# State-space norm and mixed output: where the second 128 tokens' transposes stand, and VectorE's order around them

## The chip, the cores and the metric

The kernel runs on one core of one Trainium2 chip. The metric is the device time of one execution in microseconds (us), the median of several runs.

## What is computed

The kernel computes two transformer blocks over 256 tokens of 1024 features. The first has a stick-breaking and a retention head mix, a mixture of 32 experts and a gated side input; the second has attention, a state-space branch, a gated mix of both and a dense feed-forward part. The change lies in the second block, between the state-space branch and the feed-forward part. Cut to that:

```python
def second_block(x, ...):
    ...
    attn_out = gqa_attention(q, k, v) @ w_attn_proj[i]
    ssd_y = ssd_branch(...)          # ends in rms_norm(y * silu(z), ssd_norm)
    ssd_out = ssd_y @ w_ssd_proj[i]
    g_attn, g_ssd = jnp.split(jax.nn.sigmoid(gates), N_BRANCH, axis=-1)
    mixed = (g_attn * attn_out + g_ssd * ssd_out) @ w_out[i]
    x = x + rms_norm(mixed, norm1_post[i])
    h2 = rms_norm(x, norm2_pre[i])
    gate, up = jnp.split(h2 @ w_gate_up[i], 2, axis=-1)
    ffn = (jax.nn.silu(gate) * up) @ w_down[i]
    return x + rms_norm(ffn, norm2_post[i])
```

## The kernel before

**Products in three parts.** Every large product is made from a high and a low part of both sides: `product` (L518) issues high by high (L520), high by low (L521) and low by high (L522). For weights ScalarE makes the high part of a piece (`split`, L1207, instruction L1210) and GpSimd the low part (L2163, four instructions of 128x512 for a piece of 1024 KB). For the activations, which TensorE transposes into PSUM, ScalarE copies the high part into XNT[0] and VectorE subtracts it from the PSUM value into XNT[1], the low part.

**Pieces and release.** The weights come in pieces in a fixed order: attn_proj 0 and 1, then ssd_proj (0,0), (0,1), (1,0), (1,1), out2 in the same four, then gate 0, up 0, gate 1 and so on. SP loads them into eight slots; `split_to(n)` makes ScalarE split all pieces up to number n, and each split waits (`w_used`) until TensorE is done with the piece four places ahead of it. `split_to` stands at fixed places of ScalarE's program, so its position among the other instructions sets when GpSimd gets a piece. GpSimd takes the pieces in order, each when its high part is there (`w_high`).

**The two blocks of tokens.** The 256 tokens are two blocks of 128, tb 0 and tb 1. `pair_group` (L589) makes one group of 512 output columns: for tb 0 both halves of the inner dimension (12 + 12 matmuls of 128x512), then the same for tb 1. It waits for the two weight pieces (`arrived`, on GpSimd's `w_low`) and, through `need_chunk`, for the low parts of its own block (`xnT` or `mixT`). The pieces are released in tb 1's turn.

**The state-space norm.** VectorE makes the normed rows NY (`norm(4, Y, NY)`, L2089, instruction L1543) one block after the other, with ScalarE's sum of squares (L1222) and root (L1224) ahead of each. TensorE's `norm_T(4)` is `block_transposes` (L534, instruction L539): for each block it waits for `xn` and transposes eight chunks into four PSUM banks from bank 0 on, with one increment of `xnT_ps` for four chunks. ScalarE's `block_evac` (L1241, instruction L1246) makes eight high parts for a block, VectorE's (L1558, instruction L1564) eight low parts. Between the norm and its low parts VectorE multiplies the attention's product by its gate, a column half at a time (L2094, `attn_out`): this reads PSUM banks 4 to 7, which ssd_proj's products then overwrite, and so TensorE waits for `attn_out` at 2 ahead of the first of them (L1132). On ScalarE the split for ssd_proj (1,0) stands ahead of the high parts, and those for (1,1) and out2 behind them.

**The mixed output.** When ssd_proj's rows of a block are complete (`first_rows` at 3 for tb 0, `w_used` for tb 1), VectorE multiplies them by their gate (L2101) and adds the attention's part (L2102, `mixed`). TensorE transposes both blocks (`block_transposes(XN, 0, "mixT_ps", "mixed", 0)`, L1135), ScalarE copies four high parts of 128x512 (L1478) and VectorE subtracts for four low parts (L2103 to L2105, instruction L1547). The products of out2 follow (L1137, L1138).

**Behind it.** ScalarE takes the squares of out2's first block (L1494), VectorE scales it (L2111) and adds it to x (L2112), then the squares of the new x (L1222), the other half of the second block (L1486) and so on lead to the next norm and to the feed-forward part.

Nothing is planned at run time: every engine follows its own written order, and semaphores hold them together.

Of the kernel before, what the change touches and what calls it, by code (L numbers as in the profile page):

```python
# [17 lines left out]
ALU = mybir.AluOpType  # L18
# [5 lines left out]
NTB = T // P  # L24
D = 1024
# [45 lines left out]
V_MIX, V_FFN, V_PLE, V_SSD, V_N1, V_N2 = (i * KC for i in range(6))  # L71
# [57 lines left out]
def build_program(nc, a, out):  # L129
# [5 lines left out]
    pieces, number = [], {}  # L135
# [41 lines left out]
    place = {k: n if n < late else n - late + base_c for k, n in number.items()}  # L177
# [18 lines left out]
    with ExitStack() as ctx:  # L196
# [5 lines left out]
        def sem(name):  # L202
            return sems[name]
# [40 lines left out]
        def area(at, n, parts=P):  # L244
            return arena[0:parts, at:at + n]

        def t3(ap, b):
            return ap.rearrange("p (b n) -> p b n", b=b)

        def banks(b, n):  # L250
            return PS[:, b:b + n, :].rearrange("p b n -> p (b n)")
# [6 lines left out]
        def pair(name, at_high, at_low, cols):  # L258
            return (parts_at(name + "_h", arena_byte + 4 * at_high, cols), parts_at(name + "_l", arena_byte + 4 * at_low, cols))

        X = area(0, 2048)
        XN = area(2048, 2048)
        XNT = pair("XNT", 4096, 6144, 2048)
# [62 lines left out]
        NY = area(8192, 2048)  # L326
# [45 lines left out]
        def block_part(ap, b):  # L372

            tb, h = divmod(b, 2)
            return ap.rearrange("p (c b n) -> p b c n", c=KC, b=NTB)[:, tb, 4 * h:4 * h + 4]
# [15 lines left out]
        NORM_BANK = (4, 4, 4, 4, 0, 0)  # L391
# [120 lines left out]
        def _(pe):  # L512
            def arrived(key):
                pe.wait_ge(sem("w_low"), number[key] + 1)
                if number[key] < FIRST_LOW:
                    pe.wait_ge(sem("first_low"), number[key] + 1)
# [7 lines left out]
            def transposes(src, bank, sem_name, ready, base):  # L524

                for tb in range(NTB):
                    pe.wait_ge(sem(ready), base + tb + 1)
                    for c in range(KC):
                        ins = nc.tensor.transpose(PS[:, bank + c // 2, (c % 2) * 256 + tb * P:(c % 2) * 256 + (tb + 1) * P],
                                                  t3(src, 2)[:, tb, c * P:(c + 1) * P], ident)  # L530
                        if tb == 1 and c % 2:
                            ins.then_inc(sem(sem_name), 1)

            def block_transposes(src, bank, sem_name, ready, base):  # L534

                for tb in range(NTB):
                    pe.wait_ge(sem(ready), base + tb + 1)
                    for c in range(KC):
                        ins = nc.tensor.transpose(PS[:, bank + 2 * tb + c // 4, (c % 4) * P:(c % 4 + 1) * P],  # L539
                                                  t3(src, 2)[:, tb, c * P:(c + 1) * P], ident)  # L540
                        if c % 4 == 3:
                            ins.then_inc(sem(sem_name), 1)
# [9 lines left out]
            def norm_T(i):  # L552
                if i == 1:
                    transposes(X, NORM_BANK[i], "xnT_ps", "x1", 0)
                elif i == 2:
                    block_transposes(X, NORM_BANK[i], "xnT_ps", "x2", 0)
                else:
                    by = block_transposes if i in (3, 4) else transposes
                    by(NY if i == 4 else XN, NORM_BANK[i], "xnT_ps", "xn", 2 * i)
# [3 lines left out]
            def takes(name, base, by_block=False):  # L563

                T_ready[:] = name, base, by_block
# [20 lines left out]
                                  [x[:, k, :] for x in w], start=c == first, stop=c == last)  # L586
                return ins

            def pair_group(tag, g, lhs, bank_of, first_rows=False):  # L589

                for tb in range(NTB):
                    for h in range(2):
                        arrived((tag, g, h))
                        ins = group_rows((tag, g, h), lhs, h, tb, bank_of(tb))
                        if tb == 1:
                            ins.then_inc(sem("w_used"), 1)
                        elif h == 1 and first_rows:
                            ins.then_inc(sem("first_rows"), 1)
# [514 lines left out]
            for v in range(len(UNITS)):  # L1113
                if v in FILL:
                    g, half = divmod(FILL.index(v), 2)
# [11 lines left out]
            half_group("attn_proj", 0, None, ATTT, lambda tb: 4 + tb, last=3)  # L1127
            pe.wait_ge(sem("across"), 8)
            half_group("attn_proj", 1, None, ATTT, lambda tb: 6 + tb, last=3)
            norm_T(4)  # L1130
            takes("xnT", 16, True)
            pe.wait_ge(sem("attn_out"), 2)  # L1132
            pair_group("ssd_proj", 0, XNT, lambda tb: 4 + 2 * tb)
            pair_group("ssd_proj", 1, XNT, lambda tb: 5 + 2 * tb, first_rows=True)
            block_transposes(XN, 0, "mixT_ps", "mixed", 0)  # L1135
            takes("mixT", 0, True)
            pair_group("out2", 0, XNT, lambda tb: 4 + 2 * tb)  # L1137
            pair_group("out2", 1, XNT, lambda tb: 5 + 2 * tb, first_rows=True)  # L1138

            norm_T(5)  # L1140
# [34 lines left out]
        def _(act):  # L1175
            link, _n = chain(act, "act_step")
# [15 lines left out]
            for at, name in SWAPPED:  # L1192
                dst, src = (x.rearrange("o (i b j) -> o i b j", i=2, b=2) for x in (bc[0:1, at:at + HD], a[name]))
# [44 lines left out]
                                                   ACT.Copy, scale=vecT[:, gain + c:gain + c + 1])  # L1238
                    ins.then_inc(sem("xnT_high"), 1)

            def block_evac(i, gain):  # L1241
                for tb in range(NTB):
                    for h in range(2):
                        act.wait_ge(sem("xnT_ps"), 4 * i + 2 * tb + h + 1)
                        for c in range(4 * h, 4 * h + 4):
                            ins = nc.scalar.activation(XNT[0][:, c * 256 + tb * P:c * 256 + (tb + 1) * P],  # L1246
                                                       PS[:, NORM_BANK[i] + 2 * tb + h, (c % 4) * P:(c % 4 + 1) * P],
                                                       ACT.Copy, scale=vecT[:, gain + c:gain + c + 1])
                        ins.then_inc(sem("xnT_high"), 1)
# [207 lines left out]
            for v in range(len(UNITS)):  # L1457
# [5 lines left out]
                if v - 1 in (FILL[1], FILL[3]):  # L1463
                    g = FILL.index(v - 1) // 2
# [6 lines left out]
            act.dma_start(N1P, a["norm1_post_2"].to_broadcast([P, D])).then_inc(sem("post1_in"), 16)  # L1471
            split_to(number[("attn_proj", 1)] + 3)
            act.wait_ge(sem("xn"), 2 * 4 + 2)
            block_evac(4, V_SSD)
            split_to(number[("ssd_proj", 1, 1)] + 2)
            for b in range(4):
                act.wait_ge(sem("mixT_ps"), b + 1)
                nc.scalar.activation(block_part(XNT[0], b), PS[:, b, :].rearrange("p (c n) -> p c n", c=4), ACT.Copy).then_inc(sem("mixT_high"), 1)  # L1478
            act.dma_start(N2P, a["norm2_post_2"].to_broadcast([P, D])).then_inc(sem("post2_in"), 16)
# [54 lines left out]
        def _(dve):  # L1534
            link, count = chain(dve, "dve_step")
            V = nc.vector
            tt, ts, stt = V.tensor_tensor, V.tensor_scalar, V.scalar_tensor_tensor
# [7 lines left out]
            def low(out, value, high):  # L1545

                return tt(out, value, high.bitcast(F32), ALU.subtract)  # L1547
# [7 lines left out]
                                  vecT[:, gain + c:gain + c + 1], XNT[0][:, cols].bitcast(F32), ALU.mult, ALU.subtract)  # L1555
                    ins.then_inc(sem("xnT"), 1)

            def block_evac(i, gain):  # L1558
                for tb in range(NTB):
                    for h in range(2):  # L1560
                        dve.wait_ge(sem("xnT_high"), 4 * i + 2 * tb + h + 1)
                        for c in range(4 * h, 4 * h + 4):
                            cols = slice(c * 256 + tb * P, c * 256 + (tb + 1) * P)
                            ins = stt(XNT[1][:, cols], PS[:, NORM_BANK[i] + 2 * tb + h, (c % 4) * P:(c % 4 + 1) * P],  # L1564
                                      vecT[:, gain + c:gain + c + 1], XNT[0][:, cols].bitcast(F32), ALU.mult, ALU.subtract)
                        ins.then_inc(sem("xnT"), 1)
# [485 lines left out]
            g4 = GATES.rearrange("p (b n) -> p b n", b=2)  # L2052
# [38 lines left out]
            for g in range(2):  # L2091
                dve.wait_ge(sem("w_used"), place[("attn_proj", g)] + 1)
                part = g4[:, :, g * 512:(g + 1) * 512]
                tt(part, part, PS[:, 4 + 2 * g:6 + 2 * g, :], ALU.mult).then_inc(sem("attn_out"), 1)  # L2094
            dve.wait_ge(sem("attn_out"), 2)
            block_evac(4, V_SSD)

            for tb, (name, n) in enumerate((("first_rows", 3), ("w_used", place[("ssd_proj", 1, 1)] + 1))):
                dve.wait_ge(sem(name), n)
                mix = XN[:, tb * D:(tb + 1) * D]  # L2100
                link(tt(mix, banks(4 + 2 * tb, 2), g4[:, tb, D:2 * D], ALU.mult))  # L2101
                tt(mix, mix, g4[:, tb, 0:D], ALU.add).then_inc(sem("mixed"), 1)  # L2102
            for b in range(4):  # L2103
                dve.wait_ge(sem("mixT_high"), b + 1)
                low(block_part(XNT[1], b), PS[:, b, :].rearrange("p (c n) -> p c n", c=4), block_part(XNT[0], b)).then_inc(sem("mixT"), 1)  # L2105

            def post_first(i, gain, signal):

# [84 lines left out]
```

## Time and profile before

| | us |
|---|---|
| median of 3 runs | 1630.44 |
| lowest and highest | 1629.87, 1630.76 |
| the profiled execution's own time | 1630.89 |
| its span | 1629.1 |
| TensorE busy in the span | 1477.9 (91%) |
| VectorE, ScalarE, GpSimd busy | 470.1, 421.2, 459.9 |

All times of a trace are in us from the start of the span. A table of windows has for each stretch: its bounds and length, then for TensorE's matmuls (PE), TensorE's weight loads (PEld), VectorE (DVE), ScalarE (ACT) and GpSimd (POOL) the busy time and the number of instructions in brackets, then the granted clock of TensorE as a share of 2.4 GHz, the share of the DMA engines and what they moved. A timeline row has start, duration, engine, line, operation, what is written from what, and the number of instructions; the bracket at its end is how long the engine sat idle ahead of it, and what ended that. The chain of waits has start, duration and the work that stood on the path. L520, L539, L1210, L1246, L1547 and L1564 are lines of helpers that several stages use, so the time tells which stage a row belongs to.

### The profile page before, as it was taken

How to read it: one execution, taken by the hardware profiler on the slowest of the kernel's cores; microseconds unless marked ns; L12 is line 12 of the kernel's file. 1: busy time of each engine (PE TensorE's matmuls, PEld its weight loads, DVE VectorE, ACT ScalarE, POOL GpSimd, SP SyncE). 2: the span in 40 equal slices, each digit the busy share in tenths (PEclk: the TensorE clock that was granted, in tenths of full speed). 3: DMA queues.
4: the chain of work that ended last, by engine and by line, in shares of the span. 5: the costliest groups of instructions: out<-in, count | busy, mean ns of one | idle time of the engine just before them, and what ended most of it. 6: DMA issues, size and time to landing. Idle time of an engine off the chain costs nothing.

```text
span 1629.1 us, 18659 instructions
## 1 busy us (share of the span) xinstructions
PE 1477.9 (91%) x7547; PEld 843.5 (52%) x7548; DVE 470.1 (29%) x806; ACT 421.2 (26%) x530; POOL 459.9 (28%) x356
## 2 busy tenths in 40 slices
PE   6998999998888989888888999887999998989998
PEld 5866633333333323333333333333798776789986
DVE  5526511211111111111111111112266286333311
ACT  5364310100101001001010010103555643354332
POOL 5924100000000000000000000003588563769994
PEclk9999899999999999999999999999999999989999
DMA  9531599999999999999999999999465331635540
GB/s 344 184 103 52 225 429 426 428 427 428 427 428 427 428 428 428 427 428 427 428 428 426 428 427 428 429 427 351 136 190 173 104 104 65 195 128 185 188 171 26
DMA packets 91171, 502.26 MB, mean 308 GB/s; under 512 B 7835, under 2 KB 38163, under 8 KB 66387
## 3 DMA queue, kind: packets, MB, share of 16 engines
q1 hardware_dynamic: 89600, 498.71, 75.8%
q10 hardware_dynamic: 1491, 2.36, 0.5%
q8 instruction: 65, 1.06, 0.3%
q14 instruction: 15, 0.12, 0.0%
HBM read 500.00 MB, written 1.05 MB: 308 GB/s over the span
## 4 chain that ended last, share of the span: by engine, by line
PE 54%; DMA 34%; DVE 5%; ACT 3%; issue 2%; POOL 1%; SPq 1%; ACTq 1%; DVEq 0%
DMA ring<-in_w_up_gate 33%; PE PS L841 14%; PE PS L520 10%; PE PS L522 9%; PE PS L521 9%; PE PS L859 4%; PE PS L810 1%; POOL w_low L2163 1%; DMA ring<-in_w_ple_gate 1%; PE PS L1094 1%; SPq L422 1%; ACT w_high L1210 1%; PE PS L848 0%; DVE arena L1843 0%; DVE arena L1846 0%
## 5 line engine op out<-in xcount | busy, mean ns | idle before, releaser
L2163 POOL TENSOR_TENSOR w_low<-ring,w_high 128x512 fp32r<-128x512 f32 (+1 forms) x352 | 459.6, 1341 | 1148.0 <-ACT w_high L1210 1147.1
L841 PE MATMUL PS<-ring,arena 128*64 128x512 f32 x2048 | 459.6, 600 | 35.4 <-DMA ring<-in_w_up_gate 35.3
L841 PEld LDWEIGHTS PS<-ring,arena 128*64 128x64 f32 x2048 | 142.3, 138 | 336.5 <-issue 268.5
L859 PE MATMUL PS<-ring,arena 128*64 128x512 f32 x1024 | 231.9, 606 | 28.0 <-ACT arena L1347 28.0
L1338 ACT ACTIVATE arena<-arena 128x512 f32<-128x512 f32 x32 | 20.1, 630 | 765.9 <-DVE arena L1840 765.9
L1210 ACT ACTIVATE w_high<-ring 128x2048 fp32r<-128x2048 f32 (+1 forms) x89 | 166.3, 1882 | 115.8 <-PE PS L522 101.3
L859 PEld LDWEIGHTS PS<-ring,arena 128*64 128x64 f32 x1024 | 74.3, 139 | 163.5 <-issue 163.5
L1840 DVE TENSOR_SCALAR arena<-PS 128x512 f32<-128x512 f32 x32 | 22.1, 692 | 470.3 <-PE PS L841 470.3
L520 PE MATMUL PS<-w_high,XNT_h 128*128 128x512 f32 (+1 forms) x336 | 135.7, 404 | 6.8 <-DVE XNT_l L1564 5.2
L520 PE MATMUL PS<-XNT_h,w_high 128*128 128x256 f32 (+1 forms) x464 | 132.2, 285 | 2.9 <-DVE XNT_l L1554 1.9
L522 PE MATMUL PS<-w_high,XNT_l 128*128 128x512 f32 (+1 forms) x336 | 132.4, 394 | 0.0
L521 PE MATMUL PS<-w_low,XNT_h 128*128 128x512 f32 (+1 forms) x336 | 132.4, 394 | 0.0
L521 PE MATMUL PS<-XNT_l,w_high 128*128 128x256 f32 (+1 forms) x464 | 131.8, 284 | 0.0
L522 PE MATMUL PS<-XNT_h,w_low 128*128 128x256 f32 (+1 forms) x464 | 131.8, 284 | 0.0
L1849 DVE COPY arena<-PS 128x512 f32<-128x512 f32 x32 | 22.1, 692 | 279.0 <-PE PS L859 279.0
L520 PEld LDWEIGHTS PS<-XNT_h,w_high 128*128 128x128 f32 (+1 forms) x464 | 87.3, 188 | 3.9 <-issue 2.5
L521 PEld LDWEIGHTS PS<-XNT_l,w_high 128*128 128x128 f32 (+1 forms) x464 | 87.4, 188 | 0.4
L522 PEld LDWEIGHTS PS<-XNT_h,w_low 128*128 128x128 f32 (+1 forms) x464 | 87.3, 188 | 0.3
L520 PEld LDWEIGHTS PS<-w_high,XNT_h 128*128 128x128 f32 x336 | 64.2, 191 | 23.2 <-issue 6.8
L521 PEld LDWEIGHTS PS<-w_low,XNT_h 128*128 128x128 f32 x336 | 64.1, 191 | 14.5 <-issue 0.7
L522 PEld LDWEIGHTS PS<-w_high,XNT_l 128*128 128x128 f32 x336 | 63.8, 190 | 14.9
L866 PE MATMUL PS<-arena 64*128 64x512 f32 x256 | 63.6, 615 | 0.0
(353 smaller groups left out, 1444.8 us busy)
## 6 DMA issues: line engine op xcount, KB each, us to landing
ring<-in_w_up_gate SPq DMA_DIRECT2D x128, 2048.0 KB, 24.3
ring<-in_w_down SPq DMA_DIRECT2D x64, 2048.0 KB, 22.2
ring<-in_w_in SPq DMA_DIRECT2D x35, 1024.0 KB, 5.9
ring<-in_w_gate_up SPq DMA_DIRECT2D x22, 1024.0 KB, 5.1
ring<-in_w_down SPq DMA_DIRECT2D x11, 1024.0 KB, 4.9
ring<-in_w_out SPq DMA_DIRECT2D x8, 1024.0 KB, 5.0
ring<-in_w_ple_gate SPq DMA_DIRECT2D x4, 1024.0 KB, 22.3
ring<-in_w_ssd_proj SPq DMA_DIRECT2D x4, 1024.0 KB, 5.0
```

Source lines behind the costliest of these rows:

```text
L422: sp.dma_start(slot(s)[:, 0:chunks * width].rearrange("p (k n) -> p k n", k=chunks), src).then_inc(landed[s], 16)
L520: nc.tensor.matmul(out, lhs[0], rhs[0], start=start, stop=False)
L521: nc.tensor.matmul(out, lhs[0], rhs[1], start=False, stop=False)
L522: return nc.tensor.matmul(out, lhs[1], rhs[0], start=False, stop=stop)
L841: ins = nc.tensor.matmul(PS[64 * (n % 2):64 * (n % 2) + 64, 4 + n // 2, :], x, w[:, n * 512:(n + 1) * 512], start=False, stop=c == KC - 1, ...
L859: ins = nc.tensor.matmul(PS[64 * n:64 * n + 64, 7, :], lhs, w[:, k, n * 512:(n + 1) * 512], start=(j, k) == (0, 0), stop=(j, k) == (1, 3))
L866: ins = nc.tensor.matmul(PS[:, 2 * tb + n, :], SPT[64 * n:64 * n + 64, tb * P:(tb + 1) * P], YS[64 * n:64 * n + 64, :], start=False, stop= ...
L1210: nc.scalar.activation(HIGH[m % BUF][:, 0:size(key)], slot(raw_slot(key))[:, 0:size(key)], ACT.Copy).then_inc(sem("w_high"), 1)
L1338: nc.scalar.activation(SIG, GLU, ACT.Sigmoid, scale=1.702).then_inc(sem(sig_out), 1)
L1840: ts(GLU, PS[:, 4, :], 7.0, None, ALU.min).then_inc(sem("glu"), 1)
L1849: V.tensor_copy(YS, PS[:, 7, :]).then_inc(sem("y_slots"), 1)
L2163: ins = nc.gpsimd.tensor_tensor(LOW[raw_slot(key)][:, at], slot(raw_slot(key))[:, at], HIGH[m % BUF][:, at].bitcast(F32), ALU.subtract)
```

## The change

TensorE: `block_transposes` takes the blocks that it is to do. The norm's first block is transposed ahead of ssd_proj's first group, the second between that group's tb 0 and tb 1; the wait for `attn_out` is split, 1 ahead of tb 0, and 2 ahead of tb 1. The mixed output's first block is transposed ahead of out2's first group, its second between tb 0 and tb 1.

ScalarE: the split for ssd_proj (1,1) comes between the high parts of the two blocks, and the splits for out2 (1,0) and (1,1) between the second and the third high part of the mixed output.

VectorE: gate product 0, the first block's low parts, gate product 1, the second block's low parts. For the mixed output: multiply and add of tb 0, multiply of tb 1, two low parts, add of tb 1, two low parts. The computation is the same.

```diff
-            def block_transposes(src, bank, sem_name, ready, base):
+            def block_transposes(src, bank, sem_name, ready, base, blocks=range(NTB)):
-                for tb in range(NTB):
+                for tb in blocks:
...
-            def pair_group(tag, g, lhs, bank_of, first_rows=False):
+            def pair_group(tag, g, lhs, bank_of, first_rows=False, between=None):
                 for tb in range(NTB):
+                    if tb == 1 and between:
+                        between()
...
-            norm_T(4)
+            def norm_4_rows(tb):
+                block_transposes(NY, NORM_BANK[4], "xnT_ps", "xn", 8, (tb,))
+
+            def second_rows():
+                norm_4_rows(1)
+                pe.wait_ge(sem("attn_out"), 2)
+
+            norm_4_rows(0)
             takes("xnT", 16, True)
-            pe.wait_ge(sem("attn_out"), 2)
-            pair_group("ssd_proj", 0, XNT, lambda tb: 4 + 2 * tb)
+            pe.wait_ge(sem("attn_out"), 1)
+            pair_group("ssd_proj", 0, XNT, lambda tb: 4 + 2 * tb, between=second_rows)
             pair_group("ssd_proj", 1, XNT, lambda tb: 5 + 2 * tb, first_rows=True)
-            block_transposes(XN, 0, "mixT_ps", "mixed", 0)
+            block_transposes(XN, 0, "mixT_ps", "mixed", 0, (0,))
             takes("mixT", 0, True)
-            pair_group("out2", 0, XNT, lambda tb: 4 + 2 * tb)
+            pair_group("out2", 0, XNT, lambda tb: 4 + 2 * tb,
+                       between=lambda: block_transposes(XN, 0, "mixT_ps", "mixed", 0, (1,)))
...
             act.wait_ge(sem("xn"), 2 * 4 + 2)
-            block_evac(4, V_SSD)
+            block_evac(4, V_SSD, (0,))
+            split_to(number[("ssd_proj", 1, 1)])
+            block_evac(4, V_SSD, (1,))
             split_to(number[("ssd_proj", 1, 1)] + 2)
             for b in range(4):
+                if b == 2:
+                    split_to(number[("out2", 1, 1)])
                 act.wait_ge(sem("mixT_ps"), b + 1)
...
                 tt(part, part, PS[:, 4 + 2 * g:6 + 2 * g, :], ALU.mult).then_inc(sem("attn_out"), 1)
+                block_evac(4, V_SSD, (g,))
             dve.wait_ge(sem("attn_out"), 2)
-            block_evac(4, V_SSD)
...
+            mix_times(0)
+            mix_plus(0)
+            mix_times(1)
+            mix_low(0)
+            mix_low(1)
+            mix_plus(1)
+            mix_low(2)
+            mix_low(3)
```

## Rows read from the trace of the kernel before

**Rows 1.** Table of windows, all engines, the stretches around the change and the rest.

```profile
core 0: us, PE busy (x) PEld busy (x) DVE busy (x) ACT busy (x) POOL busy (x), PEclk, DMA share, GB/s
1367.70:1373.50 5.80, 2.22 (x18) 1.75 (x17) 5.17 (x10) 5.61 (x15) 2.40 (x2) 1.00 0.70 270
...
1397.50:1401.10 3.60, 1.90 (x18) 1.66 (x16) 3.36 (x4) 1.25 (x3) 0.00 (x0) 1.00 1.08 365
1401.10:1423.50 22.40, 22.40 (x99) 17.89 (x96) 5.23 (x6) 10.63 (x13) 19.60 (x16) 1.00 0.48 153
...
1434.90:1629.10 194.20, 188.53 (x1320) 176.07 (x1320) 47.28 (x47) 71.77 (x58) 161.66 (x124) 0.98 0.42 141
```

**Rows 2.** Chain of waits, 1369.9 to 1373.5 us: start, duration, work.

```profile
1369.93 2.27 DVE arena L2094 x2
1372.22 1.14 DVE XNT_l L1564 x4
```

**Rows 3.** Timeline of ScalarE and TensorE at the state-space norm.

```profile
1369.10 1.92 ACT L1210 ACTIVATE w_high<-ring 128x2048 fp32r<-128x2048 f32 x1 [0.16 <-issue]
1370.93 4.21 ACT L1246 ACTIVATE XNT_h<-PS,vecT 128x128 fp32r<-128x128 f32 x16
...
1369.98 1.09 PE L539 MATMUL PS<-cst,arena 128*128 128x128 f32 x8 [0.42 <-DVE arena L1543]
1373.50 0.47 PE L520 MATMUL PS<-w_high,XNT_h 128*128 128x512 f32 x1 [2.42 <-DVE XNT_l L1564]
```

**Rows 4.** Timeline at an earlier norm with the same helpers, ScalarE and VectorE.

```profile
1134.84 4.23 ACT L1246 ACTIVATE XNT_h<-PS,vecT 128x128 fp32r<-128x128 f32 x16
...
1136.09 4.23 DVE L1564 SCALAR_TENSOR_TENSOR XNT_l<-PS,vecT,XNT_h 128x128 fp32r<-128x128 f32 x16 [2.61 <-ACT XNT_h L1246]
```

**Rows 5.** Timeline at the mixed output: TensorE, VectorE, ScalarE.

```profile
1397.50 1.03 PE L539 MATMUL PS<-cst,arena 128*128 128x128 f32 x8
1400.24 1.09 PE L539 MATMUL PS<-cst,arena 128*128 128x128 f32 x8 [1.70 <-DVE arena L2102]
1401.09 0.48 PE L520 MATMUL PS<-w_high,XNT_h 128*128 128x512 f32 x1
...
1398.96 1.22 DVE L2102 TENSOR_TENSOR arena<-arena 128x1024 f32<-128x1024 f32 x1
...
1401.57 1.29 DVE L1547 TENSOR_TENSOR XNT_l<-PS,XNT_h 128x512 fp32r<-128x512 f32 x2 [0.18 <-ACT XNT_h L1478]
...
1400.94 0.60 ACT L1478 ACTIVATE XNT_h<-PS 128x512 fp32r<-128x512 f32 x1 [1.71 <-PE PS L539]
```

**Rows 6.** Timeline behind out2's first products, and adds elsewhere: GpSimd, ScalarE, VectorE.

```profile
1403.90 20.06 POOL L2163 TENSOR_TENSOR w_low<-ring,w_high 128x512 fp32r<-128x512 f32 x16 [7.14 <-ACT w_high L1210]
...
1409.77 1.92 ACT L1210 ACTIVATE w_high<-ring 128x2048 fp32r<-128x2048 f32 x1 [4.14 <-PE PS L522]
...
1425.07 1.06 ACT L1222 ACTIVATE arena<-arena 128x1024 f32<-128x1024 f32 x1 [4.59 <-DVE arena L2112]
...
1426.46 0.58 ACT L1486 ACTIVATE arena<-PS 128x512 f32<-128x512 f32 x1
...
1393.37 2.24 DVE L2102 TENSOR_TENSOR arena<-arena 128x1024 f32<-128x1024 f32 x1
...
1421.29 3.75 DVE L2112 TENSOR_TENSOR arena<-arena 128x1024 f32<-128x1024 f32 x1
...
1620.99 1.22 DVE L2112 TENSOR_TENSOR arena<-arena 128x1024 f32<-128x1024 f32 x1
```

**Rows 7.** Table of windows, columns as in Rows 1, for the granted clock.

```profile
1374.10:1377.20 3.10, 3.10 (x9) 2.39 (x8) 2.35 (x10) 2.83 (x6) 2.17 (x3) 0.50 0.00 0
...
157.10:162.20 5.10, 1.09 (x8) 0.86 (x8) 3.58 (x4) 2.54 (x6) 5.10 (x5) 1.00 0.00 0
162.30:165.40 3.10, 3.10 (x7) 2.46 (x8) 3.07 (x2) 0.00 (x0) 3.10 (x2) 0.50 0.00 0
...
1401.10:1405.00 3.90, 3.90 (x20) 3.17 (x18) 1.57 (x3) 3.90 (x4) 1.10 (x1) 1.00 0.74 237
```

More of the change, by code:

```diff
@@ L1239, in norm_evac, with block_evac @@
                     ins.then_inc(sem("xnT_high"), 1)
-            def block_evac(i, gain):
-                for tb in range(NTB):
+            def block_evac(i, gain, blocks=range(NTB)):
+                for tb in blocks:
                     for h in range(2):
@@ L1556, in norm_evac, with block_evac @@
                     ins.then_inc(sem("xnT"), 1)
-            def block_evac(i, gain):
-                for tb in range(NTB):
+            def block_evac(i, gain, blocks=range(NTB)):
+                for tb in blocks:
                     for h in range(2):
@@ L2094, in _, with mix_times, mix_plus, mix_low @@
                 tt(part, part, PS[:, 4 + 2 * g:6 + 2 * g, :], ALU.mult).then_inc(sem("attn_out"), 1)
+                block_evac(4, V_SSD, (g,))
             dve.wait_ge(sem("attn_out"), 2)
-            block_evac(4, V_SSD)
-            for tb, (name, n) in enumerate((("first_rows", 3), ("w_used", place[("ssd_proj", 1, 1)] + 1))):
+            def mix_times(tb):
+                name, n = (("first_rows", 3), ("w_used", place[("ssd_proj", 1, 1)] + 1))[tb]
                 dve.wait_ge(sem(name), n)
+                link(tt(XN[:, tb * D:(tb + 1) * D], banks(4 + 2 * tb, 2), g4[:, tb, D:2 * D], ALU.mult))
+            def mix_plus(tb):
                 mix = XN[:, tb * D:(tb + 1) * D]
-                link(tt(mix, banks(4 + 2 * tb, 2), g4[:, tb, D:2 * D], ALU.mult))
                 tt(mix, mix, g4[:, tb, 0:D], ALU.add).then_inc(sem("mixed"), 1)
-            for b in range(4):
+            def mix_low(b):
                 dve.wait_ge(sem("mixT_high"), b + 1)
                 low(block_part(XNT[1], b), PS[:, b, :].rearrange("p (c n) -> p c n", c=4), block_part(XNT[0], b)).then_inc(sem("mixT"), 1)
+            mix_times(0)
[6 more added lines that the diff above has]
+            mix_low(3)
             def post_first(i, gain, signal):
```

## The prediction

> **What bounds the kernel now.** The change touches two short stretches of the second block, so the question is what ends last there, not which engine is busiest over the span. I read the table of windows first [rows 1]: between 1367.7 and 1373.5 us TensorE has no products for 5.80 us (the norm), between 1397.5 and 1401.1 none for 3.60 us (the mixed output). The products that follow each stretch run without a gap: 96 in 22.40 us, 0.233 us apart. From 1434.9 on TensorE is busy for 188.5 of 194.2 us, so what is gained or lost before that point reaches the end one for one.
>
> Then the chain of waits through the first stretch [rows 2]: the two gate products on VectorE (L2094, 2.27 us), then four low parts (L1564, 1.14 us), then TensorE at 1373.50. Read alone this says that VectorE is last. The timeline of the other engines beside it [rows 3] says more: ScalarE makes the high parts from 1370.93 on, right behind a weight split of 1.92 us that began at 1369.10. TensorE's second eight transposes (1369.98) lie in time in which it would wait anyway: they are free.
>
> **The change, part by part.** In the norm TensorE now transposes only the first 128 tokens, waits for one gate product, makes the first tokens' 24 products, and then transposes the second 128 tokens. VectorE does one gate product, eight low parts, the other gate product, eight low parts.
>
> Start of the first products. The second gate product goes from ahead of the low parts to behind them, which takes half of 2.27 us, 1.1 us, off VectorE's chain. What is late next: the low parts also wait for four high parts. At another norm with nothing in VectorE's way its low parts begin 1.25 us after ScalarE's high parts [rows 4]. Here that is 1370.93 + 1.25 = 1372.18, and they began at 1372.22 [rows 2]. So ScalarE is behind VectorE by 0.04 us only, and the start moves by at most that: I take 0. Its split and its first high parts are where they were.
>
> The hole behind the first 24 products. The eight transposes now stand between products, and the second tokens' products need their high and low parts, which nothing has made ahead. From transposes to ScalarE's first copy: 1400.94 - 1400.24 = 0.70 us [rows 5]; high to low 1.25 [rows 4]; low to product 1373.50 - 1372.22 = 1.28 [rows 2, 3]. Sum 3.2 us, of which some 0.9 us are the transposes and 2.4 us a wait. Before, this work stood under the first tokens' products. Cost: +3.2 us. Bounds: 0.9 us, were the copies somehow covered, and 3.3 us with the first hand-off at 1.29. I take 3.2: all three terms are rows of the same instructions. The second gate product (1.1 us) is behind the first eight low parts and is over well before; the wait for it costs nothing, since some 5.6 us of products cover it. ScalarE's split for ("ssd_proj", 1, 1) moves ahead of the second tokens' high parts, into the time of the first products; its piece has its use only two groups on, so GpSimd's work for it changes nothing.
>
> Start of out2. Before, TensorE sent eight transposes at 1397.50, waited for the second multiply and add on VectorE, sent eight more at 1400.24 and began at 1401.09: 3.59 us [rows 5]. Now the add of the second tokens is behind two low parts. VectorE is free of the multiply at 1398.96 (1.46 us in). The high part is there by then: 0.70 us for the hand-off and 0.6 for the copy, 1.3 us. The low part takes 0.66 us (two in 1.29), the hand-off to TensorE 0.14 (1.28 less the 1.14 of the four low parts [rows 2]): 1.46 + 0.66 + 0.14 = 2.26 us. Gain: -1.33 us. The add, 1.2 to 2.2 us [rows 6], follows the second low part and has the rest of 5.6 us of products as cover.
>
> The hole in out2. Transposes again stand between the first and the second tokens: 0.70 + 0.63 to the low part + 0.66 + 0.14 = 2.1 us [rows 2, 5] of delay for TensorE. Whether it reaches the end hangs on what follows. After out2's first tokens ScalarE takes squares, and VectorE adds x (L2112). That add began 20.2 us after out2's first product, took 3.75 us, and was over at 1425.04; the same instruction at the end of the kernel took 1.22 [rows 6]. In between GpSimd had 16 low-part instructions in one row from 1403.90, 20.06 us long, to 1423.96, and the add ends 1.08 us after it. So it waited for GpSimd, and ScalarE's next square waited for it (4.59 us idle [rows 6]). The change makes the splits for ("out2", 1, 0) and (1, 1) earlier, between high parts 1 and 2, so that GpSimd is through with both before it needs the next. It then waits for ("gate", 0), whose split followed its release at 8.68 us after the first product (1409.77); with the hole at 10.8, plus 1.92 for the split, GpSimd starts at 12.8, and eight instructions of 1.254 us (20.06 over 16) end at 22.8. The add is due at 20.2 + 2.1 = 22.3, waits 0.5 us and ends 1.08 us after GpSimd: at 23.9, and before it was 23.95. TensorE's own end, 22.4 + 2.1 = 24.5 plus 0.3 for the hand-off, is ahead of ScalarE's L1486, which stood at 25.4 [rows 6]. So the second hole is covered by a wait that shrinks. Cost: 0; without this cover, 2.1 us.
>
> The Trainium skill (SBUF — State Buffer, section on two separate sides) says that a VectorE instruction with two SBUF inputs and a GpSimd one that reads SBUF lock the port, and "the other fully blocks". The trace agrees for L2112, but by the row at 1393.37, 2.24 us, one can also get through between GpSimd's instructions; were the port shared instead of locked, the add would still be slow for its 0.5 us of overlap only.
>
> The Trainium skill (TensorE: Matmul & The Clock Gate, section on each phase of a matmul) says that TensorE pulls weight loads ahead and that matmuls "themselves stay in program order". That speaks against this change: no product of the second tokens could pass the transposes. The trace shows the same, each L539 group with products strictly behind it; the sum above has no overlap in it.
>
> SP's loads wait for the pieces' release and shift with TensorE; no load is moved past another.
>
> **The sum.** 3.23 - 1.33 + 0 = +1.9 us. On the profiled execution, 1630.89 us (span 1629.1), that is 1632.8; that execution is 0.45 us above the median of 1630.44, so 1632.3 us as the median.
>
> **Rivals.** (a) *The clock falls in the new hole.* The granted clock went to 0.50 (1.2 GHz) for 3.1 us behind the norm, and so it did after 157.1 to 162.2 us, where TensorE had eight transposes in 5.1 us; in and after the 3.6 us at 1397.5, with sixteen, it stayed at 1.00 [rows 1, 7]. The new hole has eight transposes in 3.2 us, shorter than any with a drop, but with more idle time (2.4 us) than the one without (1.7). At half the clock products take up to twice as long, so 3.1 us of it cost up to 1.55 us: I take 1.5, so 1633.8. The longer wait ahead of the first products may also bring the present drop forward from 1374.1 to 1373.5, 0.3 us more.
>
> (b) *The x add isn't relieved.* GpSimd would have to run as far past the add's start as before, for instance because its two pieces for out2 are not earlier; the hole of 2.1 us then counts: 1634.4. It decides from the point where GpSimd's last low part ends over 3 us behind the add's start. Against it: the release of ("gate", 0) fixes GpSimd's end. With (a) as well, 1635.8.
>
> (c) *The holes are hidden, and VectorE was last.* Then the transposes alone move (+0.9), the second gate product saves 1.1 and out2 starts 1.33 earlier: -1.6 us, 1628.9. For it: the chain names VectorE. Against it: 1372.18 for ScalarE, and copies that can't begin before the transposes. Only a saving of twice that would be measured as faster.
>
> **How the numbers follow.** A measurement of this kernel can tell about 0.2% (3.3 us) from no change. Forecast 0.52; (a) alone 0.24; (b) alone 0.12; both 0.05; (c) 0.07. Slower by over 0.2% are (b), both, half of (a), and a little of the forecast's own spread (0.03): 0.32. Faster: 0.04, from (c) with more than I can find. Within: 0.64. The range is 1630.8 to 1634.9: below, the forecast with the spread of the runs and a hole that is 1 us shorter; above, (a) and (b) singly with 0.5 us. It leaves out (c) and both together.
>
> **What would show it.** Right: the first product of ssd_proj still about 1.3 us behind the first low part; L539 in four groups, each pair with products between; an idle time of TensorE of some 2.3 us ahead of ssd_proj's second tokens and 1.2 ahead of out2's; out2 starting 2.3 us after its transposes; L2112 at 1.6 us instead of 3.75. Wrong: first products over 0.5 us earlier relative to the norm's end, a hole under 2 us, a granted clock of 0.50 right behind the new hole, or L2112 still over 3 us.

## The result, and the profile after

The changed kernel takes 1634.25 us (median of 14 runs, 1631.97 to 1635.82) where the kernel before takes 1630.72 in the same comparison (14 runs, 1629.51 to 1632.51). The ratio is 1.0018, 95% interval 1.0011 to 1.0025: 2.9 us slower, 1.8 to 4.1. (The two medians lie 3.5 us apart, the two means 3.1. Every "ratio" below is the recorded estimate with its interval, and a difference in us of whole times is worked out from it.) The time lies inside the range of the prediction and within the 0.2% that was called no change; the difference is 1.0 us above the forecast of 1.9. By the interval the change costs something, and it gains nothing.

The profiled execution of the changed kernel took 1635.04 us, with a span of 1633.2. To see what the change did in it, I take the stretch from the state-space norm's first normed rows (VectorE, L1543 before, L1557 after) to the feed-forward part's second normed rows (L2134, L2164). Everything that the change touches lies inside. Timeline of VectorE, the kernel before, start and duration first:

```profile
1367.66 0.75 DVE L1543 TENSOR_SCALAR arena<-arena,stat 128x1024 f32<-128x1024 f32 x1
...
1431.47 0.75 DVE L2134 TENSOR_SCALAR arena<-arena,stat 128x1024 f32<-128x1024 f32 x1
```

The same of the changed kernel:

```profile
1369.61 0.75 DVE L1557 TENSOR_SCALAR arena<-arena,stat 128x1024 f32<-128x1024 f32 x1
...
1435.18 0.75 DVE L2164 TENSOR_SCALAR arena<-arena,stat 128x1024 f32<-128x1024 f32 x1
```

63.81 us before, 65.57 after: +1.76. The other 1.95 us of this pair lie ahead of the stretch, and 0.4 behind it; the runs below show that these vary between executions of one program.

TensorE's timeline, the changed kernel, from the norm to out2's second tokens (the bracket is the idle time ahead):

```profile
1370.41 1.09 PE L539 MATMUL PS<-cst,arena 128*128 128x128 f32 x8 [0.73 <-DVE arena L1557]
1375.29 0.77 PE L520 MATMUL PS<-w_high,XNT_h 128*128 128x512 f32 x1 [3.78 <-DVE XNT_l L1578]
...
1382.48 1.03 PE L539 MATMUL PS<-cst,arena 128*128 128x128 f32 x8
1385.56 0.47 PE L520 MATMUL PS<-w_high,XNT_h 128*128 128x512 f32 x1 [2.05 <-DVE XNT_l L1578]
...
1402.44 1.04 PE L539 MATMUL PS<-cst,arena 128*128 128x128 f32 x8
1404.74 0.47 PE L520 MATMUL PS<-w_high,XNT_h 128*128 128x512 f32 x1 [1.26 <-DVE XNT_l L1561]
...
1410.41 1.04 PE L539 MATMUL PS<-cst,arena 128*128 128x128 f32 x8
1412.52 0.47 PE L520 MATMUL PS<-w_high,XNT_h 128*128 128x512 f32 x1 [1.07 <-DVE XNT_l L1561]
```

The four groups of transposes are there, each with a wait behind it. Against [rows 3]: the first product stands 5.68 us behind the first normed rows, 5.84 before, so the start has moved by 0.16 us. The first hole, 1382.48 to 1385.56, is 3.08 us; it wasn't there before. Out2 starts 2.30 us behind its first transposes, 3.59 before [rows 5]. Its own hole is 2.11 us.

The chain of waits at the norm, the changed kernel, names another engine than it did before [rows 2]:

```profile
1371.95 0.91 issue
1372.86 1.13 ACT XNT_h L1256 x4
...
1374.02 1.14 DVE XNT_l L1578 x4
```

ScalarE's four high parts stand on the path where the second gate product stood. They end 4.38 us behind the first normed rows, where the gate product ended at 4.54. Behind out2's first products, VectorE and GpSimd against [rows 6]:

```profile
1427.11 1.63 DVE L2142 TENSOR_TENSOR arena<-arena 128x1024 f32<-128x1024 f32 x1
...
1417.58 10.08 POOL L2193 TENSOR_TENSOR w_low<-ring,w_high 128x512 fp32r<-128x512 f32 x8 [1.38 <-ACT w_high L1220]
```

GpSimd's low parts have a break where it waits for gate (0)'s split. They end at 1427.66, and the add to x ends at 1428.74, 1.08 us later, as before. The add takes 1.63 us instead of 3.75.

### The profile page after: what moved, and what is told of

Read it like the earlier page. It is cut to its first block, busy times and chain, and to the rows that moved or that the text cites. A ratio compares the mean times of both kernels' runs of the same rounds, so it can differ in the third digit from the quotient of the medians.

```text
span 1633.2 us, 18660 instructions
## 1 busy us (share of the span) xinstructions
PE 1482.7 (91%) x7547; PEld 844.9 (52%) x7548; DVE 469.3 (29%) x806; ACT 421.6 (26%) x530; POOL 459.2 (28%) x356
## 4 chain that ended last, share of the span: by engine, by line
PE 58%; DMA 29%; DVE 5%; ACT 3%; issue 2%; POOL 1%; SPq 1%; ACTq 1%; DVEq 0%
DMA ring<-in_w_up_gate 28%; PE PS L843 16%; PE PS L520 9%; PE PS L521 9%; PE PS L522 9%; PE PS L861 6%; PE PS L812 1%; POOL w_low L2193 1%; DMA ring<-in_w_ple_gate 1%; SPq L422 1%; PE PS L1096 1%; PE PS L850 1%; ACT w_high L1220 1%; DVE arena L1860 1%; DVE arena L1857 1%
```

## The experiments

The theory is the prediction's sum (H): a hole at the norm, a start that ScalarE holds, an earlier out2, and a second hole that the shorter wait of the add to x covers. Its claim about the start, that ScalarE's high parts arrive as late as VectorE does, is theory S in two of the expectations. The rivals are the clock (C), a VectorE that was last (V), and an add that isn't relieved (N). In the edits, `...` stands for lines as in the changed kernel. Stretch means the one above: 63.81 us before.

**The two parts, each alone.** The norm's part, with the mixed output as before:

```diff
-            block_transposes(XN, 0, "mixT_ps", "mixed", 0, (0,))
+            block_transposes(XN, 0, "mixT_ps", "mixed", 0)
...
-                       between=lambda: block_transposes(XN, 0, "mixT_ps", "mixed", 0, (1,)))
...
-                if b == 2:
-                    split_to(number[("out2", 1, 1)])
```

> The state-space norm's part of the change alone; the mixed output as before. Theory H (hole): TensorE stands 3.1 us between the first and the second tokens' products of ssd_proj, and starts the first product no earlier; +3.0 us (2.8 to 3.2) against before, and the stages behind it as before. Theory C (clock): the same hole, and in some executions the granted clock falls behind it, up to 1.5 us more; a median of +3.5 us or more, and a wider spread than before. Theory V (VectorE was last): the first product 1.1 us earlier, +1.9 us.

Measured: ratio 1.0030 (1.0018 to 1.0042), 1635.55 us; stretch 66.78 us, +2.97. The first product stands 5.69 us behind the first normed rows, and the profile has no low clock behind the hole. The mixed output's part, with the norm as before:

```diff
-            norm_4_rows(0)
+            norm_T(4)
             takes("xnT", 16, True)
-            pe.wait_ge(sem("attn_out"), 1)
-            pair_group("ssd_proj", 0, XNT, lambda tb: 4 + 2 * tb, between=second_rows)
+            pe.wait_ge(sem("attn_out"), 2)
+            pair_group("ssd_proj", 0, XNT, lambda tb: 4 + 2 * tb)
...
-                block_evac(4, V_SSD, (g,))
             dve.wait_ge(sem("attn_out"), 2)
+            block_evac(4, V_SSD)
```

> The mixed output's part of the change alone; the norm as before. Theory H with relief: out2 starts 2.3 us behind its first transposes (3.6 before), a hole of 2.1 us between its first and second tokens, and VectorE's add to x takes 1.6 us instead of 3.75, so that the second hole costs nothing: -1.3 us. Theory N (no relief): the add still takes over 3 us: +0.8 us.

Measured: ratio 0.9999 (0.9990 to 1.0007), 1630.52 us; stretch 62.50 us, -1.31. The add to x, timeline of VectorE:

```profile
1421.60 1.61 DVE L2140 TENSOR_TENSOR arena<-arena 128x1024 f32<-128x1024 f32 x1
```

What follows: in the stretches the parts add up, 2.97 - 1.31 = 1.66 against 1.76. The hole costs what it is long; out2's is covered. V falls by the first product, which has not moved by 1.1 us, and N by the add at 1.61 us. The whole times say more than the stretches: +4.9 us for the norm's part (2.9 to 6.9), and for the second part nothing clear of noise; its interval (-1.6 to +1.1 us) only just holds -1.3. That gap comes back in most of the runs, and is taken up under what these comparisons can tell.

**The place of ScalarE's splits.** mix_alone without

```diff
-                if b == 2:
-                    split_to(number[("out2", 1, 1)])
```

> mix_alone without the earlier splits for out2 (1,0) and (1,1): they stand again behind all four high parts of the mixed output. Theory H (GpSimd's last low part decides when VectorE's add to x gets through): GpSimd starts these pieces some 4 us later than in mix_alone and ends later than the add is due by 4 us or more, so the add takes over 4 us and the part loses its gain: +1 to +5 us against mix_alone in the stretch from the norm to the feed-forward part. Rival: the splits' place is of no weight, because the release of gate (0) sets the pace: as mix_alone, the add at 1.6 us.

Measured: ratio 1.0040 (1.0025 to 1.0055), 1636.68 us; stretch 68.80 us, 6.3 above mix_alone and so over the expected 5. Timelines of VectorE, ScalarE, GpSimd and TensorE:

```profile
1425.04 4.77 DVE L2138 TENSOR_TENSOR arena<-arena 128x1024 f32<-128x1024 f32 x1
...
1406.78 5.52 ACT L1220 ACTIVATE w_high<-ring 128x2048 fp32r<-128x2048 f32 x3
...
1408.77 19.96 POOL L2189 TENSOR_TENSOR w_low<-ring,w_high 128x512 fp32r<-128x512 f32 x16 [12.33 <-ACT w_high L1220]
...
1413.87 0.50 PE L520 MATMUL PS<-w_high,XNT_h 128*128 128x512 f32 x1 [0.76 <-POOL w_low L2189]
1418.82 0.50 PE L520 MATMUL PS<-w_high,XNT_h 128*128 128x512 f32 x1 [1.89 <-POOL w_low L2189]
```

GpSimd starts at 1408.77, ends at 1428.73, and the add ends 1.08 us behind it, as in the two kernels above. What the expectation missed is that TensorE itself waits for these low parts, twice, 2.65 us. So the two moved lines carry the part: left behind all four high parts, of which the last two now come late, ScalarE's splits would cost more than the whole change does.

**VectorE's order alone, then ScalarE's with it.** Both blocks transposed ahead, as before; VectorE's new order, and TensorE's wait for the second gate product between the tokens. ScalarE's split for ssd_proj (1,1) stays between the high parts of the two blocks, as in the changed kernel:

```diff
+            def second_rows():
+                pe.wait_ge(sem("attn_out"), 2)
...
+            norm_T(4)
             takes("xnT", 16, True)
+            pe.wait_ge(sem("attn_out"), 1)
+            pair_group("ssd_proj", 0, XNT, lambda tb: 4 + 2 * tb, between=second_rows)
```

> The kernel before with VectorE's new order at the norm alone (one gate product, eight low parts, the other, eight low parts) and TensorE's wait for the second gate product moved between the first and second tokens; both blocks are transposed ahead as before, the mixed output as before. Theory S (ScalarE's high parts are 0.04 us behind VectorE): the first product starts at the same distance from the norm, within 0.1 us, and the stretch is as long as before. Theory V (VectorE was last): 1.1 us earlier.

Measured: ratio 1.0004 (0.9995 to 1.0013), 1631.50 us; stretch 63.65 us, -0.16; first product 5.68 us behind the first normed rows, as in the changed kernel. Then, in addition, ScalarE's split behind the first high parts:

```diff
-            split_to(number[("attn_proj", 1)] + 3)
             act.wait_ge(sem("xn"), 2 * 4 + 2)
             block_evac(4, V_SSD, (0,))
             split_to(number[("ssd_proj", 1, 1)])
```

> As vector_order, and ScalarE's split for ssd_proj (1,0) moved from ahead of the norm's first eight high parts to behind them. Theory S: now both engines are ready earlier; the high parts start as soon as both normed blocks are there, the first product some 1.0 us earlier than before, no hole: the stretch 1.0 us shorter than before. Theory V: no more than vector_order gives.

Measured: ratio 0.9992 (0.9982 to 1.0001), 1629.37 us; stretch 61.31 us, -2.50, more than twice the expected 1.0. Timeline of TensorE at the first product:

```profile
1373.63 0.47 PE L520 MATMUL PS<-w_high,XNT_h 128*128 128x512 f32 x1 [1.34 <-DVE XNT_l L1573]
```

The window behind it (columns as in Rows 1):

```profile
1373.70:1376.80 3.10, 3.10 (x14) 2.51 (x15) 1.94 (x5) 3.10 (x2) 1.56 (x2) 1.00 0.37 151
```

The first product is 4.75 us behind the first normed rows, 1.09 earlier than before: S is right, V is not, and VectorE's order alone was worth 0.16 us while ScalarE held the start. ScalarE's order alone was not run. Of the other 1.4 us, 1.2 lie in the 96 products up to the mixed output's transposes (22.82 us instead of 24.00) and are the clock. Before, the products behind the norm ran 3.1 us at 0.50 [rows 7]; with TensorE's last idle time at 1.34 us instead of 2.42 they run at 1.00. The clock gives back some 0.3 us more than those 1.2, and an add takes them away: the mixed output's first add takes 4.30 us here instead of 2.24, ends at 1396.40, and the transposes that wait for it start at 1396.45, where TensorE was free at 1396.17.

**The clock behind the hole.** Eight matmuls more in TensorE's wait, whose result nothing reads, once with the norm's part alone and once with the whole change:

```diff
                 norm_4_rows(1)
+                w = split_view(("ssd_proj", 0, 0))[0]
+                for _ in range(8):
+                    nc.tensor.matmul(PS[:, 5, :], XNT[0][:, 0:P], w[:, 0, :], start=True, stop=True)
                 pe.wait_ge(sem("attn_out"), 2)
```

> As norm_alone, and behind the second tokens' transposes TensorE makes eight more matmuls of 128x512 (1.9 us) into a PSUM bank that nothing reads, in the time in which it waits for the second tokens' low parts. Theory H: the same time as norm_alone within 0.3 us. Theory C: faster than norm_alone by 0.5 to 1 us, with a narrower spread, since the clock can't fall behind a filled hole.

> The changed kernel with eight matmuls of 128x512 (1.9 us), whose result nothing reads, behind the second tokens' transposes at the norm. Theory C (in some executions the granted clock falls behind the hole of 3.1 us): no low clock behind the filled hole in the profile, a median 0.5 to 1.5 us below the changed kernel's, about 1632.5 to 1633.5. Theory H alone: the same median as the changed kernel within its interval.

And the changed kernel itself twice more:

> The changed kernel once more, beside its two parts. Theory H: the sum of the parts, +1.7 us. Theory C: the sum plus the drops behind the hole, +2.5 to +3 us. If the sum of the two parts is measured at +1.7 and this one at +3, the parts act on each other, and both theories are short.

> The changed kernel a third time, for the filled one's comparison and for one more look at the clock behind the hole. Theory C: a low clock behind the hole in some of the profiles of this kernel, and the stretch then 3.3 us longer than before, and 1.8 us where there is none; the median lies between, +2 to +3 us.

Measured: norm_alone_filled 1.0016 (1.0005 to 1.0026), 1634.22 us, stretch 66.75. after_filled 1.0016 (1.0007 to 1.0025), 1634.40 us, stretch 65.59. after_again 1.0017 (1.0008 to 1.0026), 1634.33 us, stretch 67.14. after_third 1.0018 (1.0008 to 1.0027), 1634.53 us, stretch 67.15. Windows of the hole and behind it (columns as in Rows 1), first the changed kernel's first profile, which has no drop:

```profile
1382.50:1385.56 3.06, 1.01 (x9) 0.80 (x8) 1.27 (x5) 2.18 (x8) 0.50 (x1) 1.00 0.00 0
1385.60:1388.60 3.00, 3.00 (x13) 2.45 (x14) 0.85 (x4) 0.00 (x0) 0.00 (x0) 1.00 0.00 0
```

after_again, the same program:

```profile
1381.53:1384.62 3.09, 1.04 (x10) 0.83 (x8) 1.28 (x5) 2.17 (x8) 0.49 (x1) 1.00 0.00 0
1384.70:1387.80 3.10, 3.10 (x8) 2.42 (x9) 0.80 (x4) 0.00 (x0) 0.00 (x0) 0.50 0.00 0
```

after_filled:

```profile
1380.65:1383.73 3.08, 2.89 (x17) 2.22 (x16) 1.27 (x5) 2.18 (x8) 0.47 (x1) 1.00 0.00 0
1383.80:1386.90 3.10, 3.10 (x14) 2.50 (x15) 0.82 (x4) 0.09 (x1) 0.00 (x0) 1.00 0.00 0
```

The hole is equally long in all three. In after_again 3.1 us behind it ran at 0.50 with 8 matmuls where 13 or 14 ran at 1.00, and the stretch is 1.57 us longer; after_third is the same (0.50, 67.15). So rival (a) is real in some executions of one program: of the four profiles with an open hole two have the drop, of the two with a filled one none. With so few profiles that could be chance. The time doesn't settle it. The filled kernels' ratios are 0.0002 (with the whole change) and 0.0014 (with the norm's part) below the open ones', with intervals of 0.001 each way; the first is under the 0.5 us that theory C asked for. How often the drop comes stays open, and so does whether the filling gains anything in the median.

**The changed kernel with covered holes.** Both second sets of transposes behind the first 12 of the first tokens' 24 products:

```diff
                     for h in range(2):
+                        if (tb, h) == (0, 1) and inside:
+                            inside()
                         arrived((tag, g, h))
```

> The changed kernel with both sets of second transposes moved once more: behind the first 12 of the first tokens' 24 products instead of behind all 24, at the norm and in out2. Theory H: the last 12 products (2.8 us) cover the way through ScalarE and VectorE (3.2 us less the transposes), so each hole shrinks to the transposes' own 0.9 to 1.1 us: norm +0.9 us instead of +3.1, mixed output -2.6 instead of -1.3; the stretch from the norm to the feed-forward part 1.5 to 2 us shorter than before, about 1629 us. Rival: the holes stay at 2 to 3 us, because something else than the products' place makes them: as the changed kernel.

Measured: ratio 1.0003 (0.9994 to 1.0012), 1631.34 us; stretch 61.99 us, -1.82, as expected and 3.6 us less than the changed kernel's. TensorE, timeline:

```profile
1377.59 1.03 PE L539 MATMUL PS<-cst,arena 128*128 128x128 f32 x8
...
1403.23 1.04 PE L539 MATMUL PS<-cst,arena 128*128 128x128 f32 x8
```

No product behind either group has an idle time ahead of it: the holes are the transposes' own time. The whole time says +0.5 us (-1.0 to +2.0), not the 1629 that the stretch would give, though the profiled execution took 1629.42; the gain of the stretch isn't shown in the median.

**Both orders, no hole at the norm, a covered one in out2.** vector_and_scalar_order with the mixed output's part and `inside` for out2; against the changed kernel:

```diff
-            norm_4_rows(0)
+            norm_T(4)
...
-                       between=lambda: block_transposes(XN, 0, "mixT_ps", "mixed", 0, (1,)))
+                       inside=lambda: block_transposes(XN, 0, "mixT_ps", "mixed", 0, (1,)))
...
-            split_to(number[("attn_proj", 1)] + 3)
             act.wait_ge(sem("xn"), 2 * 4 + 2)
```

> vector_and_scalar_order and the mixed output's part of the change, with the second tokens' transposes inside the first tokens' products of out2 (behind the first 12 of 24) instead of behind them. Theory H: no hole at the norm (-1.0 us), out2 starts 1.3 us earlier, its second hole shrinks from 2.1 us to the transposes' 0.9, and the add to x is due 1.2 us earlier, with GpSimd's pieces earlier by as much: -1.0 - 1.3 - 1.2 = -3.5 us in the stretch, 1627 us. Rival: the add to x stays where it was because GpSimd's end does: -2.3 us.

Measured: ratio 0.9975 (0.9966 to 0.9984): 4.1 us faster than the kernel before (2.6 to 5.5), clear of noise, and the fastest of all. The median is 1627.64 us against 1630.90. Stretch 58.94 us, -4.87. The norm gives 2.3 of it up to out2's first transposes (27.58 us from the first normed rows, 29.84 before): the earlier start and the clock, which stays at 1.00. The rest, 2.6, is the mixed output's: 1.3 + 1.2 were expected. The rival, an add that stays where it was, falls; VectorE and GpSimd, timeline:

```profile
1419.73 1.63 DVE L2142 TENSOR_TENSOR arena<-arena 128x1024 f32<-128x1024 f32 x1
...
1400.09 20.18 POOL L2193 TENSOR_TENSOR w_low<-ring,w_high 128x512 fp32r<-128x512 f32 x16 [4.80 <-ACT w_high L1221]
```

**What these comparisons can tell.** The kernel before against itself:

> The kernel before once more, with a profile: ratio 1.000 within 0.1%, which shows what these comparisons can tell. The stretch from the norm's first normed rows to the feed-forward part's is 63.8 us again within 0.2; what lies ahead of it (1367.7 us to the norm in the first profile, 1368.6 and 1369.6 in the changed kernel's) varies by 1 to 2 us between executions whatever the kernel.

Measured: ratio 1.0000 (0.9991 to 1.0009); stretch 63.78 us against 63.81. Its norm begins at 1366.65 us, and in the other thirteen profiles between 1367.14 and 1369.61, three profiles of the changed kernel alone at 1367.26, 1368.63 and 1369.61. One program scatters by as much as all of them, so this stands ahead of the change; it is why a stretch repeats to 0.03 us where a ratio has 1.5 us either way. The three profiled stretches of the changed kernel are 1.76, 3.33 and 3.34 us longer than before, 2.8 in the mean. The three timed ratios are 1.0018, 1.0017 and 1.0018, that is 2.8 to 2.9 us.

That these agree does not show that the drop of the clock is the difference, for there is a rival that no run tested. Put each ratio beside its own stretch: of the eight altered kernels whose norm has no hole, or a filled or covered one, seven have a whole time 0.8 to 2.3 us above what the stretch says (the changed kernel filled: +2.6 against +1.78; mix_alone: -0.2 against -1.31; after_inside: +0.5 against -1.82), and one is 0.3 us below. The kernel before against itself shows no such gap. All but after_inside's are within their noise, and kernels timed together share their runs of before, but they point one way. So something outside the stretch may cost every altered program about 1 us, and 1.76 + 1 would give the changed kernel's +2.9 us with hardly any drop. Where that microsecond would stand was not found.

## Why the prediction was right, point by point

**The start of the first products.** Taken at 0, bounded by 0.04 us; measured 0.16 earlier (5.84 to 5.68). The step held: vector_order has it alone, and vector_and_scalar_order shows the 1.1 us that VectorE's order is worth once ScalarE makes way. The bound was 0.1 us too tight, because it took the hand-off from ScalarE to VectorE at another norm's 1.25 us. Here it was 1.29 before and is 1.16 in the changed kernel (1372.86 to 1374.02), which is 0.13 of the 0.16.

**The hole at the norm.** 3.2 forecast, 3.08 measured, 3.0 in the stretch of norm_alone with the start. The first term was a row of the mixed output's copies, the second of an earlier norm, the third of this norm; the product behind them waits for exactly these steps. In the changed kernel the first hand-off, 1382.48 to 1383.11, is 0.63 instead of 0.70, the second 1.18, the third 1.27.

**The start of out2.** 2.26 forecast, 2.30 measured.

**The hole in out2 and its cover.** 2.1 forecast, 2.11 measured; cost 0 by the sum. GpSimd was to start gate (0) 12.8 us behind out2's first product and end at 22.8; it did so at 12.84 and 22.92. The add to x was put at 1.6 us and took 1.63, ended by GpSimd as said. mix_alone's -1.31 against the forecast -1.33 confirms both at once, and mix_late_splits shows what the cover rests on. The Trainium skill (SBUF — State Buffer, section on two separate sides) has a lock that is held "for the whole instruction", and no sharing of the port. The trace agrees as far as the add ends only behind GpSimd, at 4.77 us too. It goes further than the page in one point: the add waited not only for the GpSimd instruction under way but for two more that began after it (1421.42 and 1422.66 in the kernel before, the add at 1421.29).

**The sum and the time.** 1.9 forecast for a stretch that measured 1.76 without a drop of the clock: every term of the sum held. The time measured +2.9, and 1634.25 us where 1632.3 was given, so 1.0 us of the difference has no term in the sum. The range holds it only because it was made wide enough for rivals (a) and (b). Two explanations are left, and the runs don't separate them. One is rival (a). The prediction gave the drop 0.29 in all and took the execution without it as the predicted time; two of three profiles of the changed kernel have it, at 1.57 us (1.5 forecast). A granted clock of 0.50 right behind the new hole was one of the prediction's own signs of being wrong, and it did come in these two. The rows of before, a stretch of 5.1 us with a drop and one of 3.6 us without, could not say where 3.1 us with eight transposes would fall; that it can go either way in one program was not considered. If this is the cause, a mix weighted by chance would have been nearer than the likelier single case. The other is the microsecond outside the stretch, which the prediction took as nothing. The whole change with the hole filled speaks for it: it measures +2.6 us with a stretch of +1.78. The norm's part with the hole filled speaks against it: it measures +2.6 us with a stretch of +2.94.

**Rivals.** (b) was shown wrong for this kernel by the add at 1.63 us, and right as a mechanism by mix_late_splits, at 4.77. (c) did not happen. after_inside makes one half of it happen, the hidden holes, and its stretch of -1.8 us is near the -1.6 of (c) by luck: the 1.1 us at the first product, the other half, did not come (it stands 5.69 us behind the first normed rows). Instead 1.3 us come from behind out2's first product (29.12 us to the stretch's end instead of 30.38), which (c) did not count. The rider to (a), that the longer wait at the norm brings the present drop forward and costs 0.3 us, found no support: the first 24 products take 7.19 us in the changed kernel and 7.21 before.

## What to carry to other kernels

Work that is moved behind a first half of products no longer covers itself: count its whole way through the other engines, here 3.1 us from the first of eight transposes to the next product, and put it where enough products are still to come. Before one engine's order is changed to start something sooner, look for the second engine that arrives with it; here VectorE's order alone gave 0.16 us, and both together 1.1 us of waiting and then some 1.2 us of clock. A stretch between two fixed instructions repeats to some 0.03 us in the profile where whole runs scatter by 3, but its drops of the clock are a matter of the execution, so look at more than one. And where the stretch and the whole time differ again and again in one direction, as here by about 1 us, the stretch is not the whole effect.

## What the runs showed of the hardware

- The granted clock behind one and the same hole of 3.1 us (transposes in the first microsecond, then 2.05 us idle) was 1.00 in two profiles and 0.50 for 3.1 us in two others; the changed kernel gave both. Behind the norm it was 0.50 in every kernel with a last idle time of 2.27 us or more and 1.00 in the two with 1.34 us.
- A VectorE addition with both inputs in SBUF can wait for several GpSimd instructions in a row, not only for the one under way. The add to x took 3.75 us with 2.7 us of GpSimd's work left and 4.77 with 3.7 left, each time ending 1.08 us behind GpSimd's last one. In vector_and_scalar_order and both_better the first add of the mixed output took 4.30 us, beside 16 low parts of GpSimd in one row; in the other kernels, where that row had a break, it took 2.15 to 2.24 [rows 6]. Where it got through in the kernel before (1393.37), GpSimd's next instruction took 2.27 us instead of 1.29. What lets it through in one case and not in the other was not tried. Timeline of VectorE and GpSimd, both_better:

```profile
1392.07 4.30 DVE L2121 TENSOR_TENSOR arena<-arena 128x1024 f32<-128x1024 f32 x1
...
1375.21 20.08 POOL L2193 TENSOR_TENSOR w_low<-ring,w_high 128x512 fp32r<-128x512 f32 x16 [17.02 <-ACT w_high L1221]
```
